# Products of constants issued by TensorE ahead of nine kinds of wait in a two-block transformer kernel

## The reference, cut to what matters

```python
# GDN: inverse of a unit lower triangular matrix per chunk of 64 and head, then a scan over chunks
t_inv = triangular_solve(eye + a, eye, left_side=True, lower=True, unit_diagonal=True)
# RWKV: the same kind of inverse in a chunked form, once per direction, then a scan of the state over chunks
s = s * w_t - sa * ak_t + v_t * k_t          # sa = s @ kk_t
y = ((y - mean) * rsqrt(var + eps)) * ln_gain + ln_bias
out = (y + bonus) * g                          # RWKV's end, then the output projection
# before the experts
h2 = rms_norm(x, norm2_gain) * (1 + scale) + shift
group, expert logits = h2 @ w_router           # router: best group, its two best experts, ranks by a running sum
```

## Time and profile before

| | |
|---|---|
| median of 3 runs | 2228.35 us (2227.21 to 2232.68) |
| time of the profiled execution | 2230.59 us |
| its span, first to last instruction | 2228.7 us |
| mean granted TensorE clock | 0.947 of 2.4 GHz |
| PE busy, VectorE busy, ScalarE busy | 91%, 41%, 22% of the span |
| HBM traffic | 330 MB, mean 148 GB/s; from 1731 us to about 2180 us 420 to 430 GB/s |

### The profile page before, as it was taken

The page is one execution under the profiler, slowest core; times in us unless marked ns, Lnnn a source line. Parts: engine busy times, 40 slices in busy tenths (PEclk is TensorE's granted clock), DMA queues, the critical chain, the costliest instruction groups (busy, mean ns, idle before and its releaser), DMA issues. The chain is left out here.

```text
span 2228.7 us, 28834 instructions
## 1 busy us (share of the span) xinstructions
PE 2019.5 (91%) x11962; PEld 1189.9 (53%) x11962; DVE 918.1 (41%) x1916; ACT 481.5 (22%) x977; POOL 103.9 (5%) x126
## 2 busy tenths in 40 slices
PE   8999999989699999997998998797877999999994
PEld 3445665536466334584694554584764555544452
DVE  6671064424642112348423677838654221111102
ACT  1000162141122002243122265225212111100101
POOL 0000000002310000000000001301200000000001
PEclk9999999999899999998999999888788999999997
DMA  4222201110011863110113010000027999999995
GB/s 161 76 76 76 76 20 32 65 47 29 20 40 34 340 245 123 57 67 29 38 52 122 19 39 29 2 16 15 2 95 304 388 424 426 424 424 423 424 426 225
DMA packets 54515, 330.32 MB, mean 148 GB/s; under 512 B 6512, under 2 KB 11248, under 8 KB 36080
## 3 DMA queue, kind: packets, MB, share of 16 engines
q1 hardware_dynamic: 53232, 324.26, 36.8%
q0 software_dynamic: 1152, 4.19, 0.5%
HBM read 311.65 MB, written 14.68 MB: 146 GB/s over the span
## 5 line engine op out<-in xcount | busy, mean ns | idle before, releaser
L3472 PE MATMUL psum<-m_ring,m_xg 128*64 128x512 f32 x1024 | 229.6, 604 | 15.7 <-issue 14.6
L552 PE MATMUL psum<-x,wring 128*128 128x512 f32 x384 | 167.1, 598 | 6.9 <-DMA wring<-in_w1f 6.9
L246 PE MATMUL psum<-h,wring 128*128 128x512 f32 (+1 forms) x416 | 164.2, 543 | 8.2 <-PEq L93 4.8
L3472 PEld LDWEIGHTS psum<-m_ring,m_xg 128*64 128x64 f32 x1024 | 78.0, 139 | 164.0 <-issue 162.7
L3457 PEld LDWEIGHTS psum<-m_sel,m_htok 128*128 128x128 f32 x1024 | 119.4, 195 | 13.7 <-issue 12.2
L552 PEld LDWEIGHTS psum<-x,wring 128*128 128x128 f32 x384 | 73.6, 192 | 99.4 <-issue 91.2
L3457 PE MATMUL psum<-m_sel,m_htok 128*128 128x128 f32 x1024 | 123.8, 280 | 1.4 <-DVE m_sel L3448 1.4
L246 PEld LDWEIGHTS psum<-h,wring 128*128 128x128 f32 x416 | 78.0, 194 | 75.0 <-issue 65.0
L3482 DVE TENSOR_TENSOR m_hid<-rstd,psum 64x512 f32<-64x512 f32 x32 | 22.1, 690 | 230.3 <-ACT rstd L3478 230.3
L3497 PE MATMUL psum<-m_ring,m_hid_t 128*64 128x512 f32 x512 | 113.4, 595 | 0.7 <-ACT m_hid_t L3600 0.7
L2029 PE MATMUL psum<-h,wring 128*128 128x512 f32 x192 | 89.7, 624 | 0.9 <-PEq L93 0.7
(11 more groups left out here) (608 smaller groups left out, 3112.4 us busy)
## 6 DMA issues: line engine op xcount, KB each, us to landing
m_ring<-in_w_gate SPq DMA_DIRECT2D x32, 2048.0 KB, 25.4
m_ring<-in_w_up SPq DMA_DIRECT2D x32, 2048.0 KB, 27.5
m_ring<-in_w_down SPq DMA_DIRECT2D x64, 1024.0 KB, 25.4
wring<-in_w1f SPq DMA_DIRECT2D x60, 512.0 KB, 3.2
ada_ring<-in_w_ada SPq DMA_DIRECT2D x12, 2048.0 KB, 9.9
wring<-in_w2f SPq DMA_DIRECT2D x31, 512.0 KB, 3.2
expert_rows<-tmp SPq DMA_DIRECT2D x16, 512.0 KB, 26.7
wring<-in_w1v SPq DMA_DIRECT2D x12, 512.0 KB, 3.2
```

The costliest lines, as they stand in the source:

```text
L246: return nc.tensor.matmul(place(t, out), lhs, rhs, start=(k == 0), stop=(k == KD - 1))
L552: m = nc.tensor.matmul(K.psum[:, banks[t % 4]], ws.weights(first + t, k), h[:, k], start=(k == 0), stop=(k == KD - 1))
L3472: m = nc.tensor.matmul(K.psum[i * SLOTS:(i + 1) * SLOTS, UP + s], W.xg[:, k, s], w[:, k], start=(k == 0), stop=(k == KD - 1))
```

## The change

A helper `beats` issues n products of the identity (stationary) and a matrix of ones (moving), 128 x 128, into 128 columns of a PSUM bank that nothing reads at that time. They have no semaphore. It is called on TensorE directly ahead of waits: in `last_norm` (14), in `invert` ahead of `packed` (40 in GDN, 32 in each RWKV direction) and behind the spreading products (0 in GDN, 9 in RWKV), in `rwkv_end` ahead of `scaled` (9) and of `gated` (28 and 6), in `rwkv_scan` ahead of `state` (6, then 3 five times) and at its end (10), and in `router` ahead of `both` (24). Nothing else is changed.

```diff
@@ last_norm, tensor
         yield 0.0
+        beats(nc, K, 6, 14)
         eng.wait_ge(sem["loaded"], 16 * len(loads))
@@
+def beats(nc, K, bank, n):
+
+    for i in range(n):
+        nc.tensor.matmul(K.psum[:, bank, 0:P], K.ident, K.ones, start=True, stop=True)
@@ invert, tensor
-def invert(nc, K, at, xt, n_batch, early, work, lanes, banks, seeds, seed_banks, apart):
+def invert(nc, K, at, xt, n_batch, early, work, lanes, banks, seeds, seed_banks, apart, idle):
...
         yield 0.0
+        beats(nc, K, banks[0], idle[0])
         for g in range(groups):
             eng.wait_ge(sem["packed"], g + 1)
...
             m.then_inc(sem["spread"], 1)
+        if idle[1]:
+            beats(nc, K, banks[0], idle[1])
@@ invert_stage (RWKV)
-    weave(nc, name, invert(..., range(4), seeds, range(4, 8), True))
+    weave(nc, name, invert(..., range(4), seeds, range(4, 8), True, (32, 9)))
@@ gated_delta (GDN)
-        (52, invert(nc, K, at, xt, 8, 0, work, 4, near, seeds, near, False)),
+        (52, invert(nc, K, at, xt, 8, 0, work, 4, near, seeds, near, False, (40, 0))),
@@ rwkv_end, tensor
         yield 0.1
+        beats(nc, K, 0, 9)
         eng.wait_ge(sem["scaled"], 2)
...
             yield 0.75 + 0.2 * m
+            beats(nc, K, 0, 6 if m else 28)
             eng.wait_ge(sem["gated"], m + 1)
@@ rwkv_scan, tensor
             for i, j in enumerate(order):
+                beats(nc, K, 4, 6 if i == 0 else 3)
                 pe.wait_ge(sem["state"], i + 1)
...
                     n += 1
+            beats(nc, K, 4, 10)
@@ router, tensor
+        beats(nc, K, 6, 24)
         eng.wait_ge(sem["both"], 1)
```

More of the change, by code:

```diff
@@ L1585, in invert_stage @@
 def invert_stage(nc, K, name, at, xt, n_batch, early, work, seeds, lanes=4):
-    weave(nc, name, invert(nc, K, at, xt, n_batch, early, work, lanes, range(4), seeds, range(4, 8), True))
+    weave(nc, name, invert(nc, K, at, xt, n_batch, early, work, lanes, range(4), seeds, range(4, 8), True, (32, 9)))
 def inverse_buffers(sb, name, lanes):
```

## The result

The changed kernel takes **2236.05 us** (median of 18 runs, 2232.87 to 2243.5); the kernel before, beside it on the same chips, 2231.26 (18 runs, 2222.46 to 2238.85). The ratio is **1.0021 [1.0011, 1.0031]**, so 4.8 us more, with 2.4 to 6.9 from the interval. It is slower by less than the 0.3% named in the prediction, yet surely not faster, and 1 us above the stated range. Forecast was -0.8 us, so the change itself was missed by 5.6 us. The remaining 2.9 us between 2227.5 and 2236.05 are no effect of the change: the kernel before stood at 2228.35 in the three runs that the prediction started from, and at 2231.26 in the 18 here.

What follows compares the result with a forecast made beforehand. TensorE bounds the kernel (busy 91%), but at the edited places it waits for VectorE, then works at the lower clock. Terms +2.7 +0.8 +2.2 -2.9 +2.7 -2.2 -1.5 -1.3 -1.3 = -0.8 us, from median 2228.35 to 2227.5; range 2220 to 2235.

Steps and rivals of the forecast that it cites:

- GDN, to the first solving step: GDN's preparation: 40 products start at `ended` with the clock down and end after `packed`; +2.7 us, bounds 0 and +3.5.
- RWKV's 32, each: RWKV's inverse preparations: 32 products ahead of `packed` start VectorE 0.2 us sooner or 1.5 to 2.4 later; +0.9 us taken.
- first scan: First RWKV scan: added products lengthen it from 9.5 to 11.1 us, more if the clock falls; +2.2 us taken.
- RWKV's end: `rwkv_end`: VectorE's wait at L2628 goes, transposes and L1353's records run faster; -2.2 us, bounds 0 and -2.9.
- last norm: Last norm: 14 products cost nothing, and each L503 takes 1.57 us at full clock; -1.5 us.
- router: Router: 24 products end 0.1 us late, then 16 records take half the time; -1.3 us.
- What follows it: ru1 after the first scan: products at the scan's end keep the clock up, so L2726 runs at full clock; -2.9 us.
- The 9 behind the spreading products: RWKV's inverses: 9 products fit the wait and may keep the clock up in the first steps; 0.5 us gain taken each.
- The experts' stream: Rival, experts' stage: the weight stream hides what `n4` wins, so -4.1 us falls away; 2231.6 us, chance 0.08.
- The blocks overrun at half clock: Slower rival, decided in the inverses' preparation: blocks run low for over 3 us and outlast waits; +10.2, 2238.5 us, chance 0.1.
- All low time counts: Rival: GDN's 12.5 us of low clock is halved, -6.2 in place of +2.7 us; 2218.6 us, chance 0.01.
- The clock stays up wherever products stand: Rival, all edited places: back-to-back full-size products hold full clock; -6.9 us, 2221.4 us, chance 0.18.

Runs made afterwards that it cites:

- the fitted counts: Changed kernel without scan products, 22 for 40 in GDN, 20 for 32 in RWKV, 6 for 9 ahead of `scaled`, 23 for 24 in router: 2223.88 us, ratio 0.9958.

## Why the prediction was wrong

What each part did within its own stage, as the change of a distance between two instructions against the profile that the prediction read (us; negative is shorter; worked out from the timelines; a scan is counted from its clearing of states 0 to the first instruction of the next stage). Kernels with a much different count at a place (20, 22 or 80 in an inverse, the 10 alone in the scans) are left out of its row.

| term | forecast | changed kernel | others with the same edit | profiles without it |
|---|---|---|---|---|
| GDN, to the first solving step | +2.7 | +1.8 | +2.8, +3.0 | -0.1 to 0 |
| RWKV's 32, each | +0.9 | -0.2, +1.8 | -0.2, +0.1, +1.4, +0.1 | 0 |
| first scan | +2.2 | +1.7 | +1.7 | -0.2 to -2.0, mean of ten -0.9 |
| ru1 to its L2752 | -2.9 | -2.9 | -2.9 | -2.9 in all |
| second scan | +2.7 | +2.8 | +2.8 | 0 to +0.8, mean +0.4 |
| RWKV's end | -2.2 | -2.6 | -2.6 | -1.1 to +0.4, mean -0.5 |
| last norm | -1.5 | -0.9 | -0.6 to -1.4 | 0 in five of seven |
| router | -1.3 | -1.5 | -1.7 to +0.2 | 0 |
| gather | -1.3 | -1.1 | -1.1 to -2.7 | -0.4 to +0.2 |

**The step that failed** is "What follows it": "the products at the scan's end fill the hole in which the clock fell. -2.9". The row of ru1 is the one that tells: ru1 reached L2752 after 12.4 us in the profile that the prediction read and after 9.5 in all 13 others, whether the kernel has products at the scan's end or not, the unchanged one too. The lower clock there was that one execution's, and with it the -2.9 was credited to the change though there was nothing to win. That the row matches the forecast to 0.1 us is luck of the profile, not a sign that the step was right. The same execution had a slow first scan as well: against the mean of ten others without products it costs 1.7 + 0.9 = +2.6 us, not +2.2. And its ru0 was a fast one (last section), which one profile could not tell either.

**Smaller misses.** The 9 behind the spreading products in RWKV were taken at -0.5 each. From the first solving step to the next stage, the seven profiles with the 9 (and 20 or 32 ahead) are on the mean 0.8 us shorter in the first direction and 0.9 in the second than six without them. Single ones differ by up to 2.3 us and overlap, so the forecast was rather too small, if anything. The last norm and the router together gave 0.5 less than forecast in the changed kernel's profile and 0.9 less in the mean of six. For the router the reason is the 7.25 us above: the term had the block end 0.1 late at full clock, and had no price for a begin at the lower one. In the last norm L504 repeats as forecast, but the first stands 0.7 us later in the stage than before; TensorE waited 0.33 us there for a load (`m_br`) after its 14 products had ended. Half of the slow spacing, 5.86 / 28, is 0.105 us and not 0.107; nothing hangs on it.

**What the terms add up to.** With the measured mean of each term less that of the profiles without it: +2.6 (GDN), -0.5 (RWKV's two inverse stages as a whole: the 32 cost +1.0 up to the first solving steps, the rest is 1.5 shorter), +2.6 and +2.4 (scans), 0 (ru1), -2.1, -1.1, -0.7 and -1.4 (the tail) are **+1.8 us**. Of the 5.6 us by which the change was missed, ru1 is thus 2.9, and the other terms change little in sum. The measured +4.8 has 2.4 to 6.9, so some 3 us (0.6 to 5.1) are not located; one profile for each kernel can't do that where the same stage without an edit differs by 1 to 4 us among executions. The same reading of the fitted counts gives -1.2 (GDN), -4.1 (RWKV's inverse stages, four profiles), -2.1, -1.2, 0 and -1.1, so -9.7 us, beside -9.4 measured.

**What was right.** The price of 0.22 us; that GDN's block can start only at `ended`, begins at half clock and overruns (+2.7 against +1.8 to +3.0); scans of 11.1 us (11.2); the end of RWKV; the last norm's spacing. That 24 just fit in the router held at full clock only. The experts' stream did not hide what `n4` wins either: from the first product behind the gather (L3472 before, L3487 after) to the program's end it is 506.1 us on the mean of the six profiles with products in the tail, and as much in the eight without. Here are 20 us of the kernel before, then of the changed kernel, from 6.4 and 6.1 us after the gather's begin (columns as in the earlier trace rows):

```profile
1718.00:1738.00 20.00, 18.89 (x109) 9.32 (x108) 1.98 (x4) 2.20 (x3) 0.00 (x0) 1.00 0.69 277
```
```profile
1722.00:1742.00 20.00, 18.89 (x108) 9.32 (x108) 2.14 (x4) 2.20 (x3) 0.00 (x0) 1.00 0.87 356
```

DMA was idle for 6.2 us before (0.31 x 20) and for 2.6 after: 3.6 us less, as much as `n4` and the gather became shorter in this profile (0.9 + 1.5 + 1.1). That fits a queue that waits for TensorE to use a tile, as the ring of 8 makes it.

**The rivals.** "The blocks overrun at half clock" had the right sign and its place, the inverses' preparation, was right for one of the two directions (1.8 of the 2.4 us) and for GDN; but its 2238.5 also rested on a slow ru1, which the changed kernel's profile does not have. "All low time counts" fell clearly: low time fell by 84 us, which by half would be 42 us, and the time rose. That is the rule which the Trainium skill, page TensorE: Matmul & The Clock Gate, section Terms, gives; this trace does not agree. "The clock stays up wherever products stand" is closest to what the fitted counts reach, 0.42 to 0.58% below before.

**What stays open.** Where those 3 us of the loss lie is not known. What sets the clock's phase in ru0, ru1 and the scans wasn't tried, nor is it settled whether transposes are better than products (their ratio overlaps that of the fitted counts).

## What to carry to other kernels

Size a block of filler products by its start (after the barrier or the semaphore that lets the engine in, not where it falls idle) and by the lower clock that it may begin with (22 products took 6.80 us in GDN, 24 in the router 5.62 or 7.25). While it ends before the awaited event it is free; what goes beyond costs 0.22 us a product. Here products directly ahead of a barrier cost 1.7 us for 10 in each scan and gave nothing back; the 21 between the scan's short steps made each scan another 1.0 us longer (11.1 against 10.1), and no gain from them showed. Before a stretch at the lower clock is credited to a change, look whether a second execution of the same kernel shows it in the same place.

## What the runs showed of the hardware

The first products of ru0 (64 rows, 512 columns) took 8.2 to 8.5 us in 12 of the 14 profiles, most of it at the lower clock, where full clock takes 5.51; the profile that the prediction read is one of the two others, the kernel without the scans' products the second. The row of the changed kernel, and its window:

```profile
1358.56 8.33 PE L2738 MATMUL psum<-p_mix,r_up 64*128 64x512 f32 x16 [0.97 <-PEq L93]
```
```profile
1357.00:1372.00 15.00, 13.93 (x35) 6.70 (x31) 9.48 (x10) 6.78 (x10) 0.00 (x0) 0.66 0.17 54
```

PE is busy for 13.93 of 15 us at a mean clock of 0.66 (the 17 us before stand at 1.00), and by the time `ri` begins the stage is 3.0 us longer than in the profile of before. That is as much as any part of this change, and no edit here aimed at it. Stretches without any edit differ as much between executions: from the begin of `gx` to GDN's preparation by 4.9 us, in the kernel before again as in others. The other surprise stands above: in GDN's preparation a run of 44 transposes brought the clock up as products do.
